# Gathered experts taken in order of token class, with their weights read through a table of expert numbers

## What is computed

```python
def hier_moe(x2d, w_grp, b_grp, w_exp, b_exp, w_gate, w_up, w_down):
    ...                                   # group by top-1, two experts in the group by top-2
    combine = jnp.sum(jax.nn.one_hot(global_idx, N_EXPERTS) * weights[..., None], axis=1)
    y = jnp.zeros_like(x2d)
    for e in range(N_EXPERTS):            # 32 experts, D_EXPERT = 256
        h = jax.nn.silu(x2d @ w_gate[e]) * (x2d @ w_up[e])
        y = y + combine[:, e:e + 1] * (h @ w_down[e])
    return y
```

## Time and profile before

| what | value |
|---|---|
| median of 3 runs | 1816.01 us (1814.91 to 1818.73) |
| span of the profiled execution, first to last instruction | 1814.4 us |
| busy: PE / PEld / DVE / ACT / POOL | 1775.0 / 1542.6 / 1203.1 / 943.0 / 117.9 us |
| mean granted TensorE clock, of full speed | 0.996 |
| read from HBM | 327.18 MB, 181 GB/s over the span |
| router and dense experts | about 238 to 286 us of the span |
| 33 blocks | about 286 to 599 us |

### The profile page before, as it was taken

One profiled execution on the slowest core, in us unless ns is written; L12 is line 12 of the kernel. 1 busy time (PEld: TensorE's weight loads), 2 busy tenths in 40 slices (PEclk: granted clock), 3 DMA queues, 4 the chain that ended last, 5 costly groups with the idle time before them and its releaser, 6 DMA issues.

```text
span 1814.4 us, 25840 instructions
## 1 busy us (share of the span) xinstructions
PE 1775.0 (98%) x10690; PEld 1542.6 (85%) x10690; DVE 1203.1 (66%) x1510; ACT 943.0 (52%) x1245; POOL 117.9 (6%) x82
## 2 busy tenths in 40 slices
PE   7999999999999999999999999999999999999999
PEld 7999888888888788889889888888888889888887
DVE  5955578777777765458977655555555797865553
ACT  6444366555555644456754644445444766455442
POOL 1423021000000000000130000000000013000000
PEclk9999999999999999999999999999999999999999
DMA  8420156999999455555323555556555551355553
GB/s 268 136 74 1 47 175 232 327 344 334 340 337 334 141 186 186 186 162 186 117 71 117 170 186 185 190 174 198 185 186 183 166 150 50 115 162 187 185 187 115
DMA packets 181157, 329.90 MB, mean 182 GB/s; under 512 B 6704, under 2 KB 149424, under 8 KB 168240
## 3 DMA queue, kind: packets, MB, share of 16 engines
q1 hardware_dynamic: 180896, 327.73, 53.9%
q0 software_dynamic: 144, 0.52, 0.1%
HBM read 327.18 MB, written 1.05 MB: 181 GB/s over the span
## 4 chain that ended last, share of the span: by engine, by line
PE 87%; DVE 8%; ACT 3%; DMA 1%; issue 1%; POOL 0%; SPq 0%; DVEq 0%
PE ps L541 83%; PE ps L544 4%; DVE rlo L1537 2%; DVE arena L1526 2%; ACT arena L2384 1%; ACT rhi L2384 1%; DMA ring<-in_w_in 1%; ACT L2384 0%; DVE small L2170 0%; DVE arena L2322 0%; DVE arena L1529 0%; DVE xnl L1526 0%; POOL arena L2964 0%; DVE arena L2272 0%; DVE arena L1736 0%
## 5 line engine op out<-in xcount | busy, mean ns | idle before, releaser
L1537 DVE TENSOR_TENSOR rlo<-ring,rhi 128x2048 fp32r<-128x2048 f32 x272 | 622.4, 2291 | 315.9 <-ACT rhi L2384 315.2
L2384 ACT ACTIVATE rhi<-ring 128x2048 fp32r<-128x2048 f32 x272 | 518.0, 1907 | 253.6 <-PE ps L541 122.0
L541 PE MATMUL ps<-rhi,xnh 128*128 128x512 f32 (+2 forms) x784 | 307.7, 393 | 0.0
L541 PE MATMUL ps<-rlo,xnh 128*128 128x512 f32 (+2 forms) x800 | 307.5, 384 | 0.0
L541 PE MATMUL ps<-rhi,xnl 128*128 128x512 f32 (+2 forms) x784 | 302.1, 385 | 0.0
L541 PE MATMUL ps<-xnh,rhi 128*128 128x256 f32 (+1 forms) x760 | 222.2, 292 | 3.6 <-DVE xnl L1526 2.7
L541 PE MATMUL ps<-xnl,rhi 128*128 128x256 f32 (+1 forms) x760 | 216.5, 285 | 0.0
L541 PE MATMUL ps<-xnh,rlo 128*128 128x256 f32 (+1 forms) x760 | 216.4, 285 | 0.0
L541 PE MATMUL ps<-rhi,hhi 128*128 128x512 f32 x544 | 204.1, 392 | 0.0
L541 PE MATMUL ps<-rhi,xwr 128*128 128x512 f32 x528 | 179.9, 403 | 1.8 <-issue 1.8
L541 PEld LDWEIGHTS ps<-rlo,xnh 128*128 128x128 f32 x800 | 150.5, 188 | 28.5 <-issue 0.7
(11 more groups left out here) (248 smaller groups left out, 2224.4 us busy)
## 6 DMA issues: line engine op xcount, KB each, us to landing
ring<-in_few_gu SPq DMA_DIRECT2D x66, 1024.0 KB, 5.0
ring<-in_w_in SPq DMA_DIRECT2D x45, 1024.0 KB, 5.3
ring<-in_ffn_w_gate SPq DMA_DIRECT2D x88, 512.0 KB, 3.9
ring<-in_ffn_w_up SPq DMA_DIRECT2D x88, 512.0 KB, 4.9
ring<-in_ffn_w_down SPq DMA_DIRECT2D x44, 1024.0 KB, 4.9
ring<-in_exp_w_down SPq DMA_DIRECT2D x35, 1024.0 KB, 4.9
ring<-in_w_out SPq DMA_DIRECT2D x20, 1024.0 KB, 4.9
ring<-in_w_in SPq DMA_DIRECT2D x4, 896.0 KB, 4.7
```

Of the source, the lines that this page charges most:

```text
L541: return e.matmul(o, lhsT, rhs, start=start, stop=stop, skip_group_check=True)
L1537: e.tensor_tensor(lo, raw, f32(hi), SUB).then_inc(*w.hit("lo", n))
L2384: return e.activation(o, x, func, **kw)
```

## The change

The 30 gathered experts are no longer taken in their own order. DVE sorts them into three classes by load: more than 128 tokens, 65 to 128, at most 64. The position in that order is called a place. The first three places (`WIDE = 3`) get two blocks of 128 slots each, on one load; the other 27 places get one. That is again 33 blocks, 30 sets of loads instead of 33. In this version the third field of every entry of `BLOCKS` is `False`, so no block is narrow: all branches under `if BLOCKS[j][2]` and `if narrow` produce no instruction (`MID` is not used either).

```diff
-NX = 3
+WIDE, MID = 3, 7
+BLOCKS = [(p, off, False) for p in range(NB) for off in ((0, 128) if p < WIDE else (0,))]
+NK = len(BLOCKS)
...
+        for j in range(NK + 1):
+            if j < NK and not BLOCKS[j][1]:
+                p = BLOCKS[j][0]
                 for half in range(2):
-                    plan(("few", i), I["few_gu"][x, half].rearrange("p (c n) -> p c n", c=8), chosen=("few_gu", chosen, half))
+                    plan(("few", p), I["few_gu"][ND + p, half].rearrange("p (c n) -> p c n", c=8), chosen=("few_gu", p, half))
+            if j and not BLOCKS[j - 1][1]:
+                p = BLOCKS[j - 1][0]
+                plan(("few_down", p), packed(I["exp_w_down"][0, ND + p], 2), split=False, chosen=("exp_w_down", p, 0))
...
+            def last_of(j):
+                return j + 1 == NK or BLOCKS[j + 1][0] != BLOCKS[j][0]
...
+                if last_of(j):
+                    spent[n] = (("few_gate", "few_up")[half], j)
```

DVE gets two new pieces, `places()` ahead of `slots()` and `starts()` behind `part(n+5)`; `slots()` loses its first three instructions and its last, and `spares()`, `valid` and `blend` are gone:

```diff
+            def places():
+                w.wait_ge("rank_mm")
+                ones = C("ones", 3 * NB)
+                flat = lambda x: x.rearrange("p c n -> p (c n)")
+                own(e.tensor_copy(load_of, PS[6][:, 64:64 + NB]))
+                ts(classes[:, 0], load_of, 128.0, None, ALU.is_gt)
+                own(ts(over64, load_of, 64.0, None, ALU.is_gt))
+                e.tensor_tensor(classes[:, 1], over64, classes[:, 0], SUB)
+                own(ts(classes[:, 2], over64, -1.0, 1.0, MUL, ADD))
+                own(e.tensor_tensor(class_load, classes, load_of[:, None, :].to_broadcast([128, 3, NB]), MUL))
+                e.tensor_tensor_scan(flat(class_cum[:, 0]), ones, flat(classes), 0.0, MUL, ADD)
+                own(e.tensor_tensor_scan(flat(class_cum[:, 1]), ones, flat(class_load), 0.0, MUL, ADD))
+                own(e.tensor_tensor(class_cum, class_cum, classes[:, None].to_broadcast([128, 2, 3, NB]), MUL))
+                own(e.tensor_reduce(place_start, class_cum.rearrange("p q c n -> p q n c"), AX.X, ADD))
+                stt(start1, place_start[:, 1], 1.0, load_of, ADD, SUB)
+                own(e.tensor_tensor(at_place, place_start[:, 0][:, None, :].to_broadcast([128, NB, NB]),
+                                    count[:, 0:NB, None].to_broadcast([128, NB, NB]), EQ))
+                own(e.tensor_tensor(at_prod, at_place, count[:, None, 0:NB].to_broadcast([128, NB, NB]), MUL))
+                own(e.tensor_reduce(by_place, at_prod, AX.X, ADD))
+                ts(expert_of[:, :], by_place, ND - 1.0, None, ADD).then_inc(*w.hit("few_ids"))
+                w.wait_ge("few_ids")
...
+            def starts():
+                own(e.tensor_tensor(at_prod, at_place, start1[:, None, :].to_broadcast([128, NB, NB]), MUL))
+                own(e.tensor_reduce(by_place, at_prod, AX.X, ADD))
+                e.tensor_tensor(fold, C("ident", 64), C("ident")[:, 64:128], ADD).then_inc(*w.hit("fold"))
+                ts(first_slot[:, 0:2 * WIDE:2], by_place[:, 0:WIDE], 1.0, None, SUB)
+                ts(first_slot[:, 1:2 * WIDE:2], by_place[:, 0:WIDE], 127.0, 512.0, ADD, ALU.min)
+                ts(first_slot[:, 2 * WIDE:], by_place[:, WIDE:], 1.0, None, SUB).then_inc(*w.hit("first_slot"))
```

SP reads the expert number of each place into a register, before the wait for the ring buffer, and every gathered load goes to an address made from it:

```diff
+                if x["chosen"] and x["chosen"][1] not in chosen_at:
+                    w.wait_ge("few_ids")
+                    k = x["chosen"][1]
+                    chosen_at[k] = e.value_load(expert_of[0:1, k:k + 1], min_val=0, max_val=31)
                 if n >= NR:
                     w.wait_ge(*spent[n - NR])
-                if x["chosen"] and x["chosen"][1] is not None:
-                    w.wait_ge("few_info")
+                if x["chosen"]:
```

```diff
+                for j in range(NK + 1):
+                    if j == 2:
+                        w.wait_ge("ys_zero")
+                    if j >= 2:
+                        few_place(j - 2)
+                    ...
+                    if j + 1 < NK:
+                        part(ld(("few", BLOCKS[j + 1][0])))
+                    if j < NK and not BLOCKS[j][2]:
+                        few_gated(j)
+                    if j + 2 < NK:
+                        few_window(j + 2)
+                    if j + 1 < NK:
+                        part(ld(("few", BLOCKS[j + 1][0]), 1))
+                    ...
+                    if j == NK:
+                        part(ld(("ffn", 0, 0)))
+                few_place(NK - 1)
```

More of the change, by code:

```diff
@@ L433, in program @@
         few_s, few_g = ([ar(o + 256 * i, 256) for i in range(2)] for o in (25088, 22528))
-        valid = [ar(25600 + 128 * x, 128) for x in range(NX)]
-        blend = v3(5632, 8, 128)
+        few_rows = [ar(23040 + 512 * i, 512) for i in range(2)]
+        fold = ar(24064, 64)
         same = ar(11130, 64).rearrange("p (t n) -> p t n", t=2)
@@ L1052, in few_product @@
                 for c in range(4):
[L1053 to L1060, removed]
+                    k = 4 * half + c
@@ L1179, in experts @@
                     down(ld(("moe_down", x)), 0, 2, hhi, hlo, "moe_down", x, k_of=lambda k: 2 * (x % 2) + k)
[L1180 to L1188, removed]
+                for j in range(NK + 1):
+                    if j < NK:
+                        w.wait_ge("xw", j)
+                        few_product(j, 0)
+                    if j:
+                        few_turn(j - 1)
+                    if j < NK:
+                        few_product(j, 1)
+                    if j == 2:
                         slots_turned()
-                    if i:
-                        few_down(i - 1)
-                    if i == 2:
+                    if j:
+                        few_down(j - 1)
+                    if j == 2:
                         slot_weights()
@@ L1918, in extras @@
                     w.wait_ge("sel_w", tt)
[L1920 to L1935, removed]
             def hf_of(id_, i):
@@ L1953, in few_place, with window @@
[L1953 to L1958, removed]
-                for half in range(2):
[L1960 to L1972, removed]
+            def window(j):
+                return bass.ds(e.value_load(first_slot[0:1, j:j + 1], min_val=0, max_val=512), 64 if BLOCKS[j][2] else 128)
@@ new lines, in few_window @@
+            def few_window(j):
+                if j >= 2:
+                    w.wait_ge("few_up", j - 2)
+                w.wait_ge("xwh", j)
+                w.wait_ge("xtl", 1)
+                hi = xwh[j % 2]
+                if BLOCKS[j][2]:
+                    e.tensor_tensor(hi[:, :, 64:128], xs[:, :, window(j)], f32(hi[:, :, 0:64]), SUB).then_inc(*w.hit("xw", j))
+                else:
+                    e.tensor_tensor(xwl[j % 2], xs[:, :, window(j)], f32(hi), SUB).then_inc(*w.hit("xw", j))
@@ new lines, in few_place @@
+            def few_place(j):
+                at = window(j)
+                if j:
+                    w.wait_ge("few_y", j - 1, 1)
+                if BLOCKS[j][2]:
+                    w.wait_ge("few_down", j, 1)
+                    e.tensor_copy(ys[:, :, at], PS[4 + 2 * (j % 2)][:, :].rearrange("p (c n) -> p c n", c=8)).then_inc(*w.hit("few_y", j, 1))
+                    return
+                for half in range(2):
+                    w.wait_ge("few_down", j, half)
+                    e.tensor_copy(ys[:, 4 * half:4 * half + 4, at], four(4 + 2 * (j % 2) + half)).then_inc(*w.hit("few_y", j, half))
```

219 lines of the change are left out of this document (123 added, 96 removed).

## The result

| kernel | median | lowest to highest | runs |
|---|---|---|---|
| before | 1816.69 us | 1814.91 to 1818.73 | 4 |
| after | 1836.00 us | 1834.02 to 1837.97 | 4 |

The ratio is 1.0105, 95% interval 1.0091 to 1.0119: 19.3 us slower. The forecast was 1816.8, with a range from 1812.5 to 1822.5. The time lies outside it.

What follows compares the result with a forecast made beforehand. The prediction took PE's own work and gaps to bound the kernel. Span 1814.4 + 3.5 (start) - 2.8 (behind the last block) = 1815.1, median 1.6 higher, given as 1816.8 us; range 1812.5 to 1822.5.

Steps and rivals of the forecast that it cites:

- PE's work in the stage stays at 33 x 9.32 us.: Steady blocks: same 33 blocks of the same 58 PE instructions; the removed loads and splits lie beside a gapless PE, worth 0.
- The same holds for the earlier loads of places 1 to 3: Steady blocks: issuing the loads of these places earlier changes nothing beside a PE without gaps, worth 0.
- The start, 3.5 us: Ahead of the blocks: places() and other added DVE work delay block 1 by 2.8 to 4.1 us, 3.5 taken.
- the forecast's own sign: Test set beforehand: prediction wrong if the start shifts by less than 2 or more than 5 us.
- GpSimd's collision: In starts(): GpSimd's second subtraction (1.3 us) also wants SBUF; if it goes first, DVE ends at 280.9, not 279.6.
- this rival: Clock falls at the start: gaps of 1.5 and about 2 us suffice, 1.7 us lost, 1818.5; chance 0.10.
- The table on SP: First gathered load waits for the table until about 270.7 and lands at 276.3; DVE's work hides it, worth 0.
- Behind the last block, 2.8 us of gain: After the blocks: fewer DVE copies save 2.2 us, a steadier clock up to 0.9 more; 2.8 taken.
- A slip in every block, 0.25: Rival: PE waits in each block for DVE's low part; 1822.4 at 0.2 us per block, 1828 at 0.4; chance 0.25.
- its mark: Sign of the slip in the steady blocks: a period of 9.4 us or more, and a gap at the thirteenth matmul.
- The added work is hidden, 0.12: Rival: DVE's idle time absorbs the start's added work, so the start costs nothing; 1811.4 us, chance 0.12.
- The median, 1816.8: Whole kernel: profiled span forecast at 1815.1, with the runs' median 1.6 us above the span; no measurable change.

Runs made afterwards that it cites:

- e5: Changed kernel with the arena and all tensors behind it back at the addresses of the kernel before: 1825.52 us, ratio 1.0044.
- e2: Kernel before with only 32 unused bytes put ahead of the arena: 1827.0 us, ratio 1.0058.
- e4: Changed kernel where the second block of the last two-block place loads its own down weights, one more load of 1 MB: 1831.05 us, ratio 1.0081.
- e3: Changed kernel where DVE copies the ranks out of their PSUM bank at once and slots() works on the copy: 1837.35 us, ratio 1.0117.
- e11: Kernel before with rhi alone shifted by 32 bytes and everything behind it by 256: 1830.11 us, ratio 1.0069.
- e9: e8 with the three 900-element passes moved behind hf_of(1, 1), first window and ACT's evictions ahead of the first split, extras() and slot weights later: 1818.43 us, ratio 1.001.
- e8: Changed kernel with the changes of e5, e3 and e4 together, and extras() moved into the block loop: 1817.42 us, ratio 1.0001.

## Why the prediction was wrong

- **"PE's work in the stage stays at 33 x 9.32 us."** The step that failed, and the largest one. The count was right, the duration was taken as fixed. With the arena 96 bytes further from the weights, the block took 9.42 (3.4 us in 33 blocks), and the forecast had no term for the 8.2 us in later stages, which it took for unchanged. Undoing the distance gave 10.5 us (e5); a distance of 32 bytes in the old kernel cost 10.3 (e2).
- **"The same holds for the earlier loads of places 1 to 3", worth 0.** The loads were early; but a down load kept for two blocks frees its buffer late, and SP's order puts two other loads behind it. The forecast followed what SP reads and waits for at the table, and not for which buffer each load waits. This took 5.0 us (e4).
- **The start, 3.5 us.** It cost 5.1, and by the forecast's own sign more than 5 us meant that it was wrong here. The passes were priced rightly (1.09 us each for 1.1 forecast), and `expert_of` was written at 271.8, 270.3 without the 1.5 us by which this execution was late before, for 270.7 forecast. GpSimd's collision came at its upper end: 2.19 us for a pass of 1.09. Missed were the PSUM bank, which only moved the gap (e3), and the clock: this rival was given 0.10. In its own terms it was right: a gap of PE, of 3.87 us and not of 2, was followed by half clock. That is about 2.5 of the 2.96 us that PE's work took longer; the rest is the distance, in 72 matmuls. The forecast took from its rows that only the longer gap had cost the clock; the trace of the kernel before also has a gap of 1.63 us, ahead of 868.36, with a granted clock of 0.58 from 868.9 to 871.0.
- **The table on SP, worth 0:** right. ACT's first split began at 277.87, when the load was there (276.3 forecast), and no wait of PE at the start names this load. The 4.4 us that the forecast gives beside the row as the Trainium skill's come from a section on DMAs that GpSimd issues; here SP issues them, and the changed kernel has a median of 5.0 again.
- **Behind the last block, 2.8 us of gain:** right, 2.7, and the clock stayed at 1.00 in the window from 618.1, behind gaps of 0.89 and 0.91 us, where it had been 0.69.
- **A slip in every block, 0.25:** it didn't happen. The period did rise above 9.4, which the forecast had named as its mark, but without the gap at the thirteenth matmul. The second half of that mark is what told the two apart: PE was busy 215.93 of 216.30 us.
- **The added work is hidden, 0.12:** it was not.
- **The median, 1816.8:** 1815.1 + 1.6 is 1816.7; the slip changes nothing.

With the right terms the sum for the profiled span is 1814.4 + 1.5 + 5.1 + 9.7 - 2.7 + 8.2 = 1836.2. Of the 19.3 us between the medians, 10.5 and 5.0 were shown by undoing their causes. Of the 3.8 that are left, 1.6 belong to the distance as well (e5's longer stall hid them); the rest is about the start without its share of distance (4.6) less the tail (2.7), which no run undoes alone.

## What to carry to other kernels

When a change adds or removes even a small tensor, compare where the large ones start: the first thing to look for is a stage whose code is untouched and whose matmuls take longer, and the cheapest trial is the old kernel with that shift and nothing else. When a load is kept for longer, ask which load waits for its buffer, and what stands behind that one in the issuing queue. And a gap that disappears without a gain was not the bound; look for where it went before taking the next one away.

## What the hardware showed that was not expected

- In this kernel a matmul with 512 streaming columns of split weights (`rhi`, `rlo`) is slower when its two operands' starts in SBUF differ by something other than a multiple of 256 bytes: 1.52 us in 234 matmuls (6.5 ns each) at a distance of 32 bytes, 1.74 at 96, 1.53 at 128, and nothing at 256 and 512. Shifting both by 32 or 128 bytes costs nothing. The 128-column matmuls of `few_down` (at 96) and the 256-column ones of e11 did not slow down.
- In the trace this looks like PE at full clock and 100% busy, in every stage that streams 512 columns of these weights past the shifted tensor. Over the whole kernel it is 10 us of 1816 at 32 bytes.
- PE went on at half clock behind gaps of 1.99, 2.00, 2.83, 3.68, 3.87 and 4.04 us. Each of them cost its own length and 1.6 to 2.9 us more where its half clock could be read from the same matmuls at both levels. But the length of the gap alone doesn't decide. In the changed kernel the same product of 48 matmuls of the second and third blocks takes 5.75 us behind a gap of 1.44 us and 6.96 behind one of 1.53, with a granted clock of 1.00 and of 0.66 in the 5 us from the gap's end:

```profile
883.42 0.44 PE L547 MATMUL ps<-cst,arena 128*128 128x128 f32 x2 [1.44 <-ACT arena L2434]
885.52 5.75 PE ps L544 x48
...
1484.49 0.44 PE L547 MATMUL ps<-cst,arena 128*128 128x128 f32 x2 [1.53 <-ACT arena L2434]
1486.91 6.96 PE ps L544 x48
```

In e9 that product takes 5.76 us behind a gap of 1.77, in e8 7.04 behind one of 1.76, and behind the 1.76 us of the earlier trace rows PE stayed at 1.00.
